# The first modulation in four parts instead of two, with c loaded and turned by itself

## The chip, the cores and the metric

One core of one Trainium2 chip runs the whole program in one launch. The metric is the device time in microseconds. Engines: PE multiplies, DVE, ACT and POOL work element by element, SP only issues transfers; transfers are also issued from ACT.

## What is computed

Two layers of a transformer on 512 latent and 256 context tokens of 1024 features. Only the first lines of layer 0 matter here:

```python
ml = (jax.nn.silu(c) @ w_mod[i] + b_mod[i])[:, None, :]
mc = jax.nn.silu(c_ctx) @ w_mod[i] + b_mod[i]
sh1, sc1, gt1, sh2, sc2, gt2 = jnp.split(ml, 6, axis=-1)
csh1, csc1, cgt1, csh2, csc2, cgt2 = jnp.split(mc, 6, axis=-1)
hl = rms_norm(xl, g_mix_pre[i]) * (1.0 + sc1) + sh1
hc = rms_norm(xc, g_mix_pre[i]) * (1.0 + csc1) + csh1
```

After them `hl` and `hc` are multiplied by the input projection `ab_w_in`, whose first part here are the values of the gated linear attention ("v0").

## The kernel before

**Precision and weights.** All products of the layers are float32 made of three products in fp32r: high part by high part, high by low, low by high. A unit of weights (0.5 MB) is loaded by SP into `w_raw` (3 places), rounded by ACT into `w_hi` (L855), and the rest is taken by POOL, or for some units by DVE, into `w_lo` (L537). The helper `feed(s)` of an engine does this for all units up to s. The unit of the stage v0 with number u serves the feature groups k = 2u and 2u + 1.

**Head.** Tokens lie in 6 tiles of 128 rows (4 latent, 2 context) in `x_res`, loaded by two transfers (L997, L998). For each tile ACT sums the squares (L844), POOL takes the root, DVE scales into `xs` (L1217), PE turns it in 8 transposes (L1863), and ACT (L1010) and DVE (L1451) copy the turned tile from PSUM to `x_t`, which holds features on partitions: 8 groups k of 128 features.

**First modulation.** Shift and scale of the mixer (the first 2048 columns of `w_mod[0]`) come as 16 tiles m of 0.5 MB in `mod_early` (8 places). They are split in two halves of 512 features for shift and scale each. Half 0 is m = 0 to 7, each one block of 128 input features. `modulation_rows` (L1824) multiplies a tile by the two columns silu(c), silu(c_ctx) in `c_pad`; four column groups of PE give four rows of results in one bank. When a half is complete, ACT copies it (L867), `modulation_columns` (L1851) turns it in two transposes, and `modulation_half` on DVE adds the bias (L1463) and forms `pre_a` = (1 + scale) * gain (L1469). Then ACT writes `h_hi` (L1032), DVE the same unrounded into `xs` (L1478, `modulate`) and the difference into `h_lo` (L1485, `modulated_low`), group after group.

The small parameters (bias rows, gains, c, c_ctx) come through one buffer, `par_rows`, with 9 transfers on one semaphore `par_in`; PE turns them at once (L2019, L2020), DVE copies them, and ACT makes `c_pad` (L1006) from them, all ahead of the first square. Products that only keep PE busy (`keep_busy`, L2025) stand before and after the first columns.

**v0.** PE runs `v0_part` for k = 0 to 7 (first pass, 18 products of 512 columns each: 6 token tiles by three products, L2044), then the same 8 groups by 160 further columns (second pass). Between them stand the tiles of half 1, four after k = 0 and four after k = 1, and its columns after k = 2:

```python
for k in range(KT):
    v0_part(k, sp("v0") + k // 2, BV * (k % 2), BV, True, k % 2 == 1, lambda t: ps(t, 0, BV))
    if k < 2:
        modulation_rows(range(KT + 4 * k, KT + 4 * k + 4))
    if k == 2:
        modulation_columns(1)
```

DVE then casts masks (L1506, L1507) and multiplies and adds the 8 tiles of the third modulation, m = 16 to 23, which is 16 operations into `la` (L1305, L1308, `add_rows("v0")`). PE sums them over partitions after v0, while DVE takes `r_tok` and `a_v` from PSUM (L1512, L1514); with these the next stage, "in0", begins. Each engine runs its own list in order; the order is the order of the code in its block.

## Time and profile before

| | |
|---|---|
| median of 3 runs | 1710.32 us (1709.58 to 1711.84) |
| the profiled execution | 1710.0 us |
| its span | 1708.2 us |
| PE busy | 1659.3 us (97%) |
| DVE, ACT, POOL busy | 744.8, 643.2, 684.6 us |
| granted clock of PE, mean | 0.996 |

The profile is of one execution. Times in its rows count from the span's start. A row gives the start, the duration, the engine, the line, the operation and out<-in; in brackets how long the engine sat idle before and what ended that. An fp32 product by 256 columns leaves two records.

### The profile page before, as it was taken

The page shows a single profiled execution, that of the slowest core. Times are in us where ns is not written, and L with a number is a line of the kernel's source. Part 1 is how long each engine was busy: PE and PEld are TensorE (multiplying, and loading weights), DVE is VectorE, ACT ScalarE, POOL GpSimd, SP SyncE. Part 2 cuts the span into 40 slices and gives each one's busy share as a digit, 9 for nine tenths or more (in the row PEclk, how much of TensorE's full clock was granted, in tenths as well). Part 3 has the DMA queues.
Part 4 walks back from the last instruction along what each step waited for, and adds up shares of the span by engine and source line. Part 5 has one row for each costly group of instructions (what it writes and reads, how often), then busy time and mean ns, then how long its engine had stood idle before and what let it go on. Part 6 is the DMA issues. An engine that isn't in the chain of part 4 may idle for free.

```text
span 1708.2 us, 25721 instructions
## 1 busy us (share of the span) xinstructions
PE 1659.3 (97%) x10146; PEld 1383.5 (81%) x10146; DVE 744.8 (44%) x1147; ACT 643.2 (38%) x1118; POOL 684.6 (40%) x453
## 2 busy tenths in 40 slices
PE   6999999998999999999999999999999999999997
PEld 4868886787887887879999878887888888888885
DVE  4836557717598644404655320016762441011103
ACT  4242126726422122223555442236763422222221
POOL 2311232048554545545641142325433544444443
PEclk9999999999999999999999999999999999999999
DMA  9742201034565655534666627342002442333331
GB/s 357 255 121 79 49 15 50 2 86 124 160 198 190 220 151 183 169 99 123 174 173 189 189 84 130 90 117 69 2 2 62 136 146 89 111 99 99 96 102 62
DMA packets 211987, 207.17 MB, mean 121 GB/s; under 512 B 16262, under 2 KB 180636, under 8 KB 211612
## 3 DMA queue, kind: packets, MB, share of 16 engines
q1 hardware_dynamic: 199208, 165.53, 32.3%
q10 hardware_dynamic: 12660, 39.99, 7.6%
q8 instruction: 82, 1.34, 0.3%
q14 instruction: 37, 0.30, 0.1%
HBM read 203.37 MB, written 2.13 MB: 120 GB/s over the span
## 4 chain that ended last, share of the span: by engine, by line
PE 89%; DVE 3%; issue 2%; POOL 2%; ACT 2%; DMA 1%; SPq 0%; DVEq 0%; POOLq 0%; ACTq 0%
PE ps L1746 45%; PE ps L1773 26%; PE ps L1929 3%; PE ps L1985 3%; PE ps L2044 3%; PE ps L1950 3%; POOL w_lo L537 2%; PE ps L1863 1%; PE ps L1824 1%; PE ps L1997 1%; ACT w_hi L855 1%; PE ps L2025 1%; DVE full L1257 1%; DMA mod_early<-in_w_mod 1%; ACT prob L957 1%
## 5 line engine op out<-in xcount | busy, mean ns | idle before, releaser
L537 POOL TENSOR_TENSOR w_lo<-w_raw,w_hi 128x1024 fp32r<-128x1024 f32 (+1 forms) x220 | 561.1, 2553 | 850.3 <-ACT w_hi L855 850.1
L1746 PE MATMUL ps<-h_hi,w_hi 128*128 128x512 f32 (+1 forms) x1488 | 496.0, 352 | 5.2 <-POOL w_lo L537 5.1
L1746 PE MATMUL ps<-h_hi,w_lo 128*128 128x512 f32 (+1 forms) x1488 | 491.6, 349 | 0.0
L1746 PE MATMUL ps<-h_lo,w_hi 128*128 128x512 f32 (+1 forms) x1488 | 490.6, 348 | 0.0
L855 ACT ACTIVATE w_hi<-w_raw 128x1024 fp32r<-128x1024 f32 (+1 forms) x273 | 286.6, 1051 | 329.4 <-PE ps L1773 282.4
L1746 PEld LDWEIGHTS ps<-h_hi,w_hi 128*128 128x128 f32 x1488 | 269.6, 189 | 49.0 <-issue 12.8
L1746 PEld LDWEIGHTS ps<-h_hi,w_lo 128*128 128x128 f32 x1488 | 269.3, 189 | 36.4
L1746 PEld LDWEIGHTS ps<-h_lo,w_hi 128*128 128x128 f32 x1488 | 269.3, 189 | 35.9
L537 DVE TENSOR_TENSOR w_lo<-w_raw,w_hi 128x1024 fp32r<-128x1024 f32 x53 | 69.7, 1316 | 195.4 <-ACT w_hi L855 195.4
L1327 DVE TENSOR_TENSOR hid_f<-silu_g,ps 128x512 f32<-128x512 f32 (+1 forms) x66 | 39.3, 595 | 253.4 <-PE ps L1746 252.9
L1773 PE MATMUL ps<-w_hi,hid_hi 128*128 128x512 f32 x440 | 136.1, 390 | 1.5 <-POOL w_lo L537 1.0
L1773 PE MATMUL ps<-w_hi,hid_lo 128*128 128x512 f32 x440 | 135.5, 389 | 0.0
L1773 PE MATMUL ps<-w_lo,hid_hi 128*128 128x512 f32 x440 | 135.5, 389 | 0.0
L928 ACT ACTIVATE hid_hi<-hid_f 128x512 fp32r<-128x512 f32 (+1 forms) x66 | 37.0, 560 | 240.9 <-DVE hid_f L1327 240.9
L1773 PEld LDWEIGHTS ps<-w_hi,hid_hi 128*128 128x128 f32 x440 | 82.2, 188 | 20.3 <-issue 2.2
L1773 PEld LDWEIGHTS ps<-w_lo,hid_hi 128*128 128x128 f32 x440 | 82.6, 188 | 17.2
L1773 PEld LDWEIGHTS ps<-w_hi,hid_lo 128*128 128x128 f32 x440 | 82.6, 188 | 17.1
L922 ACT ACTIVATE silu_g<-ps 128x512 f32<-128x512 f32 (+1 forms) x66 | 34.6, 524 | 145.0 <-PE ps L1746 144.7
L957 ACT ACTIVATE prob<-prob,negm 128x512 f32<-128x512 f32 (+2 forms) x112 | 78.2, 699 | 28.0 <-DVE negm L1367 19.1
L1773 PE MATMUL ps<-w_hi,h_hi 128*128 128x512 f32 x256 | 80.0, 394 | 3.3 <-POOL w_lo L537 3.3
L1773 PE MATMUL ps<-w_lo,h_hi 128*128 128x512 f32 x256 | 78.9, 390 | 0.0
L1773 PE MATMUL ps<-w_hi,h_lo 128*128 128x512 f32 x256 | 78.9, 389 | 0.0
(228 smaller groups left out, 1916.4 us busy)
## 6 DMA issues: line engine op xcount, KB each, us to landing
w_raw<-in_w_ffn_in SPq DMA_DIRECT2D x132, 512.0 KB, 3.9
w_raw<-in_w_ffn_out SPq DMA_DIRECT2D x66, 512.0 KB, 3.6
mod_raw<-in_w_mod ACTq DMA_DIRECT2D x42, 512.0 KB, 4.6
w_raw<-in_na_w_in SPq DMA_DIRECT2D x32, 512.0 KB, 3.8
mod_early<-in_w_mod SPq DMA_DIRECT2D x30, 512.0 KB, 10.5
full<-in_w_mod ACTq DMA_DIRECT2D x15, 512.0 KB, 5.3
w_raw<-in_ab_w_in SPq DMA_DIRECT2D x18, 256.0 KB, 7.5
w_raw<-in_ab_w_in SPq DMA_DIRECT2D x9, 512.0 KB, 4.3
```

Of the source, the lines that this page charges most:

```text
L537: eng.tensor_tensor(w_lo[:, u % RING, 0:width], w_raw[:, u % RAW, 0:width], w_hi[:, u % RING, 0:width].bitcast(F32), ALU.subtract).then_in ...
L855: act.activation(w_hi[:, u % RING, 0:width], w_raw[:, u % RAW, 0:width], ACT.Copy).then_inc(w_hi_done, 1)
L922: act.activation(silu_g[:, f % 2, 0:width], ps(2 * (f % 2), 0, width), ACT.Silu)\
L928: act.activation(hid_hi[:, j * width:(j + 1) * width], hid_f[:, f % 2, 0:width], ACT.Copy)\
L957: act.activation(prob[:, p % 2, x, 0:n], prob[:, p % 2, x, 0:n], ACT.Exp, bias=negm[:, c % 2, head:head + 1], scale=SCALE if layer == 0 el ...
L1327: dve.tensor_tensor(hid_f[:, f % 2, 0:width], silu_g[:, f % 2, 0:width], ps(2 * (f % 2) + 1, 0, width), ALU.mult).then_inc(ff_full, 1)
L1746: mm = pe.matmul(o[0], sta(x, o), mov(y, o), start=first and n == 0, stop=last and n == 2)
L1773: mm = pe.matmul(o, act(x, k, t), w[y][:, c:c + n], start=k == 0 and (x, y) == ("hi", "hi") and first_in_bank(name, i, c), stop=k == n_uni ...
L1929: mm = pe.matmul(ps(scores_bank(layer, p, x), at, at + width), q, kk[:, col:col + width], start=at % 512 == 0, stop=i == len(runs[x]) - 1, ...
L1950: mm = pe.transpose(ps(4 + x, j * P, (j + 1) * P), probs(p, x, j), ident[:])
L1985: mm = pe.matmul(ps(bank, at, at + P, 64 * x, 64 * x + 64), value_tile(p, x, j), turned_probs(layer, p)[:, x, j * P:(j + 1) * P], start=j ...
L2044: mm = pe.matmul(place(t), h_act(x, k, t), w[y][:, at:at + width], start=k == 0 and (x, y) == ("hi", "hi") and (first or t in (0, 3)), sto ...
```

## The change

`QT` = 4 quarters of 256 features for shift and scale each take the place of two halves. A tile m of a quarter holds two blocks of 128 input features (a "pair"), loaded by two transfers whose contiguous pieces are 1 KB instead of 2 KB. Quarter 0 (m = 0 to 3) is loaded first of all on SP's queue and used in the head, between the turned tiles; quarters 1 to 3 are loaded before units 1 to 3 and multiplied after k = 0, 2 and 4. Their columns stand inside k = 1, 3 and 5, before the third token tile. Each bank now holds two partial sums per result, so the turn is a product by a part of the identity that adds them: four products with 64 columns for two transposes. On ACT the copy of a quarter stands ahead of the rounding of the next unit. c and c_ctx get a buffer `c_rows`, their own transfers, issued first on ACT's queue, and their own turn; the other parameters are turned at the head's end. Tokens come in six transfers, one per tile, each with its own semaphore. The sink's copy and the w_lo of unit 0 move back on DVE. `nth(b)` only renumbers the waits of the later modulations. The core of the diff:

```diff
+QT = 4
...
             if m < 2 * KT:
-                both = a["w_mod"][0, k * P:(k + 1) * P, 0:2 * D].rearrange("p (i h n) -> p i h n", i=2, h=2)
-                eng.dma_start(mod_place(m).rearrange("p (i n) -> p i n", i=2), both[:, :, b])\
-                    .then_inc(mod_landing(m)[0], 16)
+                q, pair = divmod(m, QT)
+                rows = a["w_mod"][0, 2 * pair * P:2 * (pair + 1) * P, 0:2 * D].rearrange("(r p) (i q n) -> q p r i n", p=P, i=2, q=QT)
+                dst = mod_place(m).rearrange("p (r i n) -> p r i n", r=2, i=2)
+                for r in range(2):
...
             sync.dma_start(ident[:], a["k_ident"]).then_inc(ident_in, 16)
+            for m in range(QT):
+                mod_load(sync, m)
...
-            for src in (a["c"].rearrange("b (r n) -> (b r) n", n=P), a["c_ctx"].rearrange("(r n) -> r n", n=P)):
-                sync.dma_start(par_rows[at:at + KT, 1, :], src).then_inc(par_in, 16)
-                at += KT
-            sync.dma_start(sink[:], a["a_sink"].partition_broadcast(P)).then_inc(par_in, 16)
-            for m in range(KT):
-                mod_load(sync, m)
+            sync.dma_start(sink[:], a["a_sink"].partition_broadcast(P)).then_inc(sink_in, 16)
             for u, parts in enumerate(units):
-                if u in (sp("v0") + 1, sp("v0") + 2):
-                    first = KT + 4 * (u - sp("v0") - 1)
-                    for m in range(first, first + 4):
+                if sp("v0") < u < sp("v0") + QT:
+                    for m in range(QT * (u - sp("v0")), QT * (u - sp("v0") + 1)):
                         mod_load(sync, m)
-                if u == sp("v0") + RAW:
+                if u == sp("v0") + QT:
                     for dst, src in ((mask_in[:, 0:LT * 2 * P], a["k_near"]), (mask_in[:, LT * 2 * P:], a["k_window"]),
                                      (tri[:].rearrange("p a n -> p (a n)"), a["k_tri"])):
...
+            def quarter_copy(q):
+                act.wait_ge(mod_used, rows_done(QT * (q + 1) - 1))
+                if q >= 2:
+                    act.wait_ge(mod_turned, q - 1)
+                act.activation(gate_b[:, q % 2, 0:256], ps(6 + (q > 0), 0, 256), ACT.Copy).then_inc(mod_copied, 1)
...
-            act.dma_start(x_res[:, 0:LT, :], a["x"][0].rearrange("(t p) d -> p t d", p=P)).then_inc(x_in, 16)
-            act.dma_start(x_res[:, LT:NT, :], a["ctx"][0].rearrange("(t p) d -> p t d", p=P)).then_inc(ctx_in, 16)
+            act.dma_start(c_rows[0:KT], a["c"].rearrange("b (r n) -> (b r) n", n=P)).then_inc(c_in, 16)
+            act.dma_start(c_rows[KT:2 * KT], a["c_ctx"].rearrange("(r n) -> r n", n=P)).then_inc(c_in, 16)
+            for t in range(NT):
+                act.dma_start(x_res[:, t, :], a["x"][0, t * P:(t + 1) * P] if t < LT else a["ctx"][0, (t - LT) * P:(t - LT + 1) * P])\
+                    .then_inc(x_in[t], 16)
...
-            act.wait_ge(par_done, 1)
+            act.wait_ge(c_turned, 1)
             act.wait_ge(c_zero, 1)
-            act.activation(c_pad[:, :, 0:2], par_col[:, 68:84].rearrange("p (v k) -> p k v", v=2), ACT.Silu)\
+            act.activation(c_pad[:, :, 0:2], ps(5, 0, 2 * KT).rearrange("p (v k) -> p k v", v=2), ACT.Silu)\
                 .then_inc(c_done, 1)
...
-                pre_square("mix0", i, range(NT), (x_in, 16) if i < LT else (ctx_in, 16))
+                pre_square("mix0", i, range(NT), (x_in[i], 16))
                 if i >= 3:
                     take_turned(i - 3)
             take_turned(3)
             take_turned(4)
+            take_turned(5)
+            quarter_copy(0)
             feed(sp("v0"))
-            take_turned(5)
-            mod_copy(0)
             act.wait_ge(pre_half, NT)
             act.wait_ge(pre_full, NT)
             for k in range(KT):
-                if k == KT // 2:
-                    mod_copy(1)
-                if k in (0, KT // 2):
-                    act.wait_ge(mod_done, 1 if k == 0 else 2)
-                    act.wait_ge(*(mod_half, 1) if k == 0 else (mod_der, 1))
+                if k % 2 == 0:
+                    act.wait_ge(mod_done, k // 2 + 1)
+                    act.wait_ge(*(mod_half, k // 2 + 1) if k < KT - 2 else (mod_der, 1))
                 for lc, cols in enumerate((slice(0, SEQ), slice(SEQ, TOK))):
                     last = act.activation(h_hi[:, k, cols], x_t[:, k, cols], ACT.Identity,
                                           bias=mod_col[:, 0, lc, k:k + 1], scale=pre_a[:, 0, lc, k:k + 1])
                 last.then_inc(*(x_hi, 1) if k < KT - 1 else (pre_hi, NT))
-                if k in (1, 3):
+                if k % 2 == 1 and k < KT - 1:
+                    quarter_copy(k // 2 + 1)
                     feed(sp("v0") + 1 + k // 2)
 
             feed(sp("in0") + 1)
...
-            dve.wait_ge(par_in, 16 * 9)
-            dve.tensor_scalar(nsink[:], sink[:], -1.0, None, ALU.mult)
-            dve.wait_ge(par_turned, 2)
-            dve.tensor_copy(bias_col[:], ps(6, 0, 96))
-            dve.tensor_copy(par_col[:], ps(7, 0, 84)).then_inc(par_done, 1)
-            dve.wait_ge(par_done, 1)
...
-            feed(sp("v0"))
+            dve.wait_ge(par_turned, 2)
+            dve.tensor_copy(bias_col[:], ps(7, 0, 96))
+            dve.tensor_copy(par_col[:], ps(1, 0, 68)).then_inc(par_done, 1)
+            dve.wait_ge(par_done, 1)
+            def quarter(q):
+                dve.wait_ge(mod_turned, q + 1)
+                rows = ps(6 * (q > 0), 0, P).rearrange("p (j i v) -> p i v j", j=2, i=2)[:, :, 0:2]
+                cols = slice(2 * q, 2 * q + 2)
+                for i in range(2):
+                    bias = bias_col[:, i * KT + 2 * q:i * KT + 2 * q + 2]
+                    bias = bass.AP(bias.tensor, bias.offset, [list(bias.ap[0]), [0, 2], [1, 2]])
+                    last = dve.tensor_tensor(mod_col[:, i, :, cols], rows[:, i], bias, ALU.add)
                 last.then_inc(mod_done, 1)
...
+                dve.wait_ge(mod_done, q + 1)
+                gain = par_col[:, cols]
+                gain = bass.AP(gain.tensor, gain.offset, [list(gain.ap[0]), [0, 2], [1, 2]])
                 dve.scalar_tensor_tensor(pre_a[:, 0, :, cols], mod_col[:, 1, :, cols], 1.0, gain, ALU.add,
-                                         ALU.mult).then_inc((mod_half, mod_der)[h], 1)
-
-            modulation_half(0)
+                                         ALU.mult).then_inc(mod_half if q < QT - 1 else mod_der, 1)
+            quarter(0)
...
-            dve.wait_ge(mod_done, 1)
-            dve.wait_ge(mod_half, 1)
             for k in range(KT + 1):
-                if k == KT // 2:
+                if k == 1:
+                    feed(sp("v0"))
+                if k:
                     modulated_low(k - 1)
-                    modulation_half(1)
-                    dve.wait_ge(mod_done, 2)
-                    dve.wait_ge(mod_der, 1)
-                if k == 1:
-                    modulated_low(0)
+                if k and k < KT and k % 2 == 0:
+                    quarter(k // 2)
+                if k < KT and k % 2 == 0:
+                    dve.wait_ge(mod_done, k // 2 + 1)
+                    dve.wait_ge(*(mod_half, k // 2 + 1) if k < KT - 2 else (mod_der, 1))
                 if k < KT:
                     modulate(k)
-                if k > 1 and k != KT // 2:
-                    modulated_low(k - 1)
+            dve.wait_ge(sink_in, 16)
+            dve.tensor_scalar(nsink[:], sink[:], -1.0, None, ALU.mult)
             dve.wait_ge(consts_in, 16 * 3)
             dve.tensor_copy(window_b[:], mask_in[:, LT * 2 * P:])
             dve.tensor_copy(near_b[:].rearrange("p t n -> p (t n)"), mask_in[:, 0:LT * 2 * P]).then_inc(masks_done, 1)
...
+            def quarter_rows(q, pairs):
+                bank = 6 + (q > 0)
+                for pair in pairs:
+                    m = QT * q + pair
+                    if pair == 0:
+                        claim(bank)
+                    pe.wait_ge(*mod_landing(m))
+                    for g in range(4):
+                        mm = pe.matmul(ps(bank, 0, 256, 32 * g, 32 * g + 32), c_pad[:, 2 * pair + g // 2, :],
+                                       mod_place(m)[:, 256 * g:256 * g + 256], start=pair == 0, stop=pair == QT - 1,
+                                       skip_group_check=True)
+                    mm.then_inc(mod_used, 1)
+                if pairs[-1] == QT - 1:
+                    read_by((bank,), (mod_copied, q + 1))
+            def quarter_columns(q):
+                bank = 6 * (q > 0)
+                claim(bank)
+                pe.wait_ge(mod_copied, q + 1)
+                for j in range(2):
+                    for r in range(2):
+                        mm = pe.matmul(ps(bank, 64 * j, 64 * j + 64), gate_b[:, q % 2, j * P:(j + 1) * P],
+                                       ident[:, 64 * r:64 * r + 64], start=r == 0, stop=r == 1, skip_group_check=True)
+                mm.then_inc(mod_turned, 1)
+                read_by((bank,), (mod_done, q + 1))
 
             def modulation_sum(b):
...
-            pe.wait_ge(par_in, 16 * 9)
             pe.wait_ge(ident_in, 16)
-            pe.transpose(ps(6, 0, 96), par_rows[0:96, 0, :], ident[0:96, 0:96]).then_inc(par_turned, 1)
-            pe.transpose(ps(7, 0, 84), par_rows[0:84, 1, :], ident[0:84, 0:84]).then_inc(par_turned, 1)
-            read_by((6, 7), (par_done, 1))
+            pe.wait_ge(c_in, 32)
+            pe.transpose(ps(5, 0, 2 * KT), c_rows[0:2 * KT], ident[0:2 * KT, 0:2 * KT]).then_inc(c_turned, 1)
+            read_by((5,), (c_done, 1))
             pe.wait_ge(c_done, 1)
             def keep_busy(bank, n):
...
-            for m in range(KT):
-                modulation_rows([m])
-                if 1 <= m <= NT:
-                    pre_turn("mix0", [m - 1])
+            for pair, turned_tiles in enumerate(((0, 1, 2), (3,), (4,), (5,))):
+                pre_turn("mix0", turned_tiles)
+                quarter_rows(0, [pair])
+            pe.wait_ge(par_in, 16 * 6)
+            pe.transpose(ps(7, 0, 96), par_rows[0:96, 0, :], ident[0:96, 0:96]).then_inc(par_turned, 1)
+            pe.transpose(ps(1, 0, 68), par_rows[0:68, 1, :], ident[0:68, 0:68]).then_inc(par_turned, 1)
+            read_by((7, 1), (par_done, 1))
             claim(7)
             keep_busy(7, 3)
-            modulation_columns(0)
+            quarter_columns(0)
...
+                    if first and k % 2 == 1 and k < KT - 1 and t == 2:
+                        quarter_columns(k // 2 + 1)
...
                 v0_part(k, sp("v0") + k // 2, BV * (k % 2), BV, True, k % 2 == 1, lambda t: ps(t, 0, BV))
-                if k < 2:
-                    modulation_rows(range(KT + 4 * k, KT + 4 * k + 4))
-                if k == 2:
-                    modulation_columns(1)
+                if k % 2 == 0 and k < KT - 2:
+                    quarter_rows(k // 2 + 1, range(QT))
```

The places, as each engine's list has them. On PE, the columns of the second part of the modulation: `ps` is PSUM, `gate_b` the copied rows, `mod_early` the modulation tiles. Before, after k = 2:

```order
L2044 MATMUL ps<-w_hi,h_lo 128x512
L1851 MATMUL ps<-ident,gate_b 128x128 x2
L2044 MATMUL ps<-w_hi,h_hi 128x512
L2044 MATMUL ps<-w_lo,h_hi 128x512
L2044 MATMUL ps<-w_hi,h_lo 128x512
```

Now, from the end of k = 0 (the value product is L2085):

```order
L1849 MATMUL ps<-mod_early,c_pad 32x256 x16
L2085 MATMUL ps<-w_hi,h_hi 128x512
L2085 MATMUL ps<-w_lo,h_hi 128x512
L2085 MATMUL ps<-w_hi,h_lo 128x512
L2085 MATMUL ps<-w_hi,h_hi 128x512
L2085 MATMUL ps<-w_lo,h_hi 128x512
L2085 MATMUL ps<-w_hi,h_lo 128x512
L1863 MATMUL ps<-ident,gate_b 128x64 x4
```

The columns moved from between two steps into the step that follows their rows, behind two token tiles, and there are three such places.

On DVE, the end of the head and the first feature groups, before:

```order
L1451 COPY x_t<-ps 128x4x128 x2
L537 TENSOR_TENSOR w_lo<-w_raw,w_hi 128x1024
L1463 TENSOR_TENSOR mod_col<-ps,bias_col 128x2x4 x2
L1469 SCALAR_TENSOR_TENSOR pre_a<-mod_col,par_col 128x2x4
L1478 TENSOR_SCALAR xs<-x_t,pre_a,mod_col 128x512
L1478 TENSOR_SCALAR xs<-x_t,pre_a,mod_col 128x256
L1485 TENSOR_TENSOR h_lo<-xs,h_hi 128x768
```

and now, up to the second quarter:

```order
L1462 COPY bias_col<-ps 128x96
L1463 COPY par_col<-ps 128x68
L1473 TENSOR_TENSOR mod_col<-ps,bias_col 128x2x2 x2
L1478 SCALAR_TENSOR_TENSOR pre_a<-mod_col,par_col 128x2x2
L1487 TENSOR_SCALAR xs<-x_t,pre_a,mod_col 128x512
L1487 TENSOR_SCALAR xs<-x_t,pre_a,mod_col 128x256
L547 TENSOR_TENSOR w_lo<-w_raw,w_hi 128x1024
L1494 TENSOR_TENSOR h_lo<-xs,h_hi 128x768
```

The parameters' copies moved from the start of the list to behind the last turned tile, and w_lo from ahead of the modulation to between the first modulated group and its h_lo.

On ACT, the first feature groups, before and then now:

```order
L1032 ACTIVATE h_hi<-x_t,mod_col,pre_a 128x512
L1032 ACTIVATE h_hi<-x_t,mod_col,pre_a 128x256
L855 ACTIVATE w_hi<-w_raw 128x1024
L1032 ACTIVATE h_hi<-x_t,mod_col,pre_a 128x512
L1032 ACTIVATE h_hi<-x_t,mod_col,pre_a 128x256
```

```order
L1044 ACTIVATE h_hi<-x_t,mod_col,pre_a 128x512
L1044 ACTIVATE h_hi<-x_t,mod_col,pre_a 128x256
L878 ACTIVATE gate_b<-ps 128x256
L861 ACTIVATE w_hi<-w_raw 128x1024
L1044 ACTIVATE h_hi<-x_t,mod_col,pre_a 128x512
```

The rounding of the next unit now stands behind the copy of a quarter, so behind PE's tiles of it.

## Rows read from the trace of the kernel before

**Rows 1.** The page's first part: busy us and share of the span, by engine.

```profile
PE 1659.3 (97%) x10146; PEld 1383.5 (81%) x10146; DVE 744.8 (44%) x1147; ACT 643.2 (38%) x1118; POOL 684.6 (40%) x453
```

**Rows 2.** The chain that ended last, to 120 us: start, us, what.

```profile
27.51 1.49 PE ps L2025 x6
...
36.78 1.86 PE ps L1824 x32
...
38.64 4.30 PE ps L2044 x18
...
49.12 0.22 PE ps L1851 x2
...
49.34 36.49 PE ps L2044 x234
```

**Rows 3.** Timeline, PE: the first value product.

```profile
32.33 0.58 PE L2044 MATMUL ps<-w_hi,h_hi 128*128 128x512 f32 x1
```

**Rows 4.** Timeline, DVE: the sums of the third modulation and what follows.

```profile
57.90 4.85 DVE L1305 TENSOR_SCALAR la<-mod_early,c_pad 128x1024 f32<-128x1024 f32 x2
...
62.67 22.39 DVE L1308 SCALAR_TENSOR_TENSOR la<-mod_early,c_pad,la 128x1024 f32<-128x1024 f32 x14
...
85.85 0.42 DVE L1512 COPY r_tok<-ps 128x96 f32<-128x96 f32 x2 [0.78 <-PE ps L2044]
```

**Rows 5.** Timeline, ACT: table load, squares, copies, rounding, h_hi.

```profile
4.45 1.28 ACT L1006 ACT_TABLE_LOAD   x1 [4.45 <-issue]
...
13.00 1.04 ACT L844 ACTIVATE junk<-x_res 128x1024 bf16<-128x1024 f32 x1
...
15.46 1.06 ACT L844 ACTIVATE junk<-x_res 128x1024 bf16<-128x1024 f32 x1
...
20.60 0.60 ACT L1010 ACTIVATE x_t<-ps 128x512 f32<-128x512 f32 x1 [0.16 <-PE ps L1863]
...
27.57 0.39 ACT L867 ACTIVATE gate_b<-ps 128x256 f32<-128x256 f32 x1
...
29.81 2.50 ACT L1032 ACTIVATE h_hi<-x_t,mod_col,pre_a 128x512 fp32r<-128x512 f32 x4 [1.85 <-DVE pre_a L1469]
...
33.48 1.06 ACT L855 ACTIVATE w_hi<-w_raw 128x1024 fp32r<-128x1024 f32 x1 [1.16 <-DMA w_raw<-in_ab_w_in]
```

**Rows 6.** DMA queues from 6 to 8 us: packets, MB, share of 16 engines.

```profile
q10 hardware_dynamic: 187, 0.75, 92.2%
...
q1 hardware_dynamic: 173, 0.05, 10.4%
```

**Rows 7.** Timeline, PE transposes; then 14 to 19 us: busy by engine, PEclk, DMA share, GB/s.

```profile
16.80 1.97 PE L1863 MATMUL ps<-ident,xs 128*128 128x128 f32 x8
...
19.47 1.09 PE L1863 MATMUL ps<-ident,xs 128*128 128x128 f32 x8
...
14.00:19.00 5.00, 4.29 (x28) 2.20 (x32) 1.70 (x3) 3.77 (x9) 3.86 (x8) 1.00 1.05 387
```

**Rows 8.** Timeline, DVE: first unit's w_lo, and modulated groups.

```profile
27.59 1.22 DVE L537 TENSOR_TENSOR w_lo<-w_raw,w_hi 128x1024 fp32r<-128x1024 f32 x1
...
29.83 0.87 DVE L1478 TENSOR_SCALAR xs<-x_t,pre_a,mod_col 128x512 f32<-128x512 f32 x2
...
31.22 0.96 DVE L1485 TENSOR_TENSOR h_lo<-xs,h_hi 128x768 fp32r<-128x768 f32 x1 [0.52 <-ACT h_hi L1032]
...
34.64 2.98 DVE L1478 TENSOR_SCALAR xs<-x_t,pre_a,mod_col 128x512 f32<-128x512 f32 x2
```

**Rows 9.** Timeline, POOL: w_lo of weight units.

```profile
34.62 2.40 POOL L537 TENSOR_TENSOR w_lo<-w_raw,w_hi 128x1024 fp32r<-128x1024 f32 x1 [11.03 <-ACT w_hi L855]
...
55.85 6.36 POOL L537 TENSOR_TENSOR w_lo<-w_raw,w_hi 128x1024 fp32r<-128x1024 f32 x2 [12.08 <-ACT w_hi L855]
```

**Rows 10.** Lines L1364 and L1305 of DVE: duration ns min/median/max.

```profile
L1364 DVE SCALAR_TENSOR_TENSOR negm<-raw_max,nsink x24: 161/161/890, 260.1 to 337.0; 128x2 f32<-128x2 f32 x24
...
L1305 DVE TENSOR_SCALAR xs<-mod_raw,c_pad x6: 746/750/2900, 454.6 to 1360.0; 128x1024 f32<-128x1024 f32 x6
```

49 lines of the change are left out of this document (21 added, 28 removed).

## The prediction

> **What bounds the kernel now.** I read the page's engine line first: PE is busy for 97% of the span [rows 1], so only stretches where PE waits, or works on something other than the products, can give time back. The chain of waits then shows the place of the change [rows 2]. Behind the tokens' transposes and the first weight tiles it is PE itself: 1.49 us of keep-busy products that begin at 27.51, when the last weight tile of the first modulation half has been multiplied, and the first value product at 32.33 [rows 3]. From there PE never waits until 85.83: value steps of 4.30 us (18 products) alternate with groups of 1.86 us (four modulation tiles), and from 49.34 on 36.49 us follow without a gap: five more steps at 4.1, to 69.8, and the second pass over the narrow columns, 16.0. At 85.85 comes a short turn over DVE (r_tok), after which the stage "in0" starts. I call the time of the first value product T: 32.33 us before.
>
> What matters for the change is how near DVE is to being late. Its 16 sums for the third modulation (la<-mod_early) start at 57.90, as soon as the modulated tiles are done, and end at 62.67 + 22.39 = 85.06, only 0.8 us before PE wants DVE at 85.85 [rows 4]. So DVE has no slack at the end of this stage, though it is busy for only 44% of the span [rows 1].
>
> **The head, up to T.** c no longer waits for the small parameters: its two 4 KB transfers are issued first. ACT then issues 6 token transfers at 0.5 us and the four gw ones (all six of before were issued when the table load began at 4.45); so I put this load (1.28 us) at 6.0 and the first square near 7.5, against 13.00 [rows 5]. Tiles: while both queues had work (6 to 8 us) the token queue moved 0.75 MB in 187 packets and the other 0.05 MB in 173, about one packet each in turn [rows 6]. Token packets stay 4 KB; the modulation packets are now 1 KB. I estimate four fifths of 387 GB/s [rows 7] for tokens: 0.52 MB in 1.7 us, first tile at 6 us, sixth near 14.5, and the 2 MB of quarter 0 at about 18.
>
> ACT's floor is 6 squares at 1.23 us (13.00 to 15.46 for two) plus 6 copies of 0.60 = 11.0 us, so 18.5. The loop over DVE and PE took 1.6 us per tile before; here the first tile is scaled at about 9.7, the first transposes take 1.97 us instead of 1.09 [rows 5, 7], and DVE needs 1.5 us per tile. I get 21.9 for the end of the last quarter-0 tile, with 18.6 as floor and 24.3 if all transposes take the slow price. From there before needed 32.33 - 27.51 = 4.8 us. New on this path: the parameter transposes and their two copies, which now stand behind the sixth tile (0.4 + 0.5 us, and 0.1 of semaphores: 1.0); column products instead of two transposes (+0.7, below); and w_lo of the first weight unit, 1.22 us on DVE, now stands between the first modulation and h_lo, where DVE had idled 0.52 (+0.7) [rows 8]. T = 21.9 + 4.8 + 2.4 = **29.1, 3.2 us earlier** (25.5 to 31.5).
>
> **The columns.** Two transposes cost PE 0.22 us [rows 2]. They become four fp32 products with 64 moving columns, three times inside the value steps. Not shown anywhere: from below 4 x 0.11 = 0.44 us; from above 8 records at the 0.25 us of the keep-busy products (six records in 1.49, with 256 columns) = 2.0. With a quarter of those columns the lower end is the nearer row; I take 0.9.
>
> **The value steps.** Call r the time at which the four tiles of a quarter are multiplied. Before, k = 0 and its group ended at 36.78 + 1.86, so r1 = T + 6.3 [rows 2]. After r, PE does two tiles of the odd step (1.4), the columns (0.9 + 0.1), four tiles (2.7): it is at the next even step at r + 5.1. ACT: copy 0.39, then w_hi of the next unit 1.06, so POOL starts that unit's w_lo at r + 1.6 and ends it at r + 4.0 (2.40 us) [rows 5, 8, 9]. In this window the columns come out (r + 2.4) and DVE must add the bias, form pre_a, modulate and subtract. What POOL does to DVE then is in the trace: the modulation of one feature group takes 0.87 us alone and took 2.98 when it started at 34.64, 0.02 us behind a w_lo on POOL; it ended with it [rows 8, 9]. Small ones too: the fused operation on raw_max and nsink takes 161 ns and once 890 [rows 10]. So I let pre_a, which reads two SBUF tiles, wait until r + 4.0: pre_a at r + 4.15, h_hi on ACT 1.25 us (2.50 for two groups), h_lo 0.96 [rows 5, 8], with 0.3 of semaphores: PE can start the even step at r + 6.65 and has stood idle 1.55 us. The Trainium skill, SBUF - State Buffer, section Who interferes with whom, says the same of this case: a VectorE instruction with two SBUF inputs, or in a two-port mode, and GpSimd lock each other out for a whole instruction; one that reads PSUM and one SBUF tile doesn't, which would leave the bias sums free. By this rule the sum is as it stands; without it for the small operation, it is rival (a).
>
> An even step with its group takes 4.30 + 1.86 us [rows 2]. So r2 = T + 19.1, r3 = T + 32.0, the last even step starts at T + 38.7, and the first pass ends at T + 46.9. Before: 69.8 - 32.33 = 37.5. **+9.4 us**, of which 1.9 is the group that was in the head, 2.5 the columns (3 x 0.9 - 0.2), 4.65 the three idle stretches, 0.35 switches between shapes. The second pass (16.0 us) is unchanged and ends at T + 62.9.
>
> **DVE at the end.** The last modulated group is done at r3 + 8.35 = T + 40.4; before it was T + 24.4, 1.15 us ahead of the sums. Sink and mask casts: 1.15. The sums took 27.2 us, and the first two of them 4.85, where such a sum takes 0.75 alone [rows 4, 10]: 3.35 us were lost to the w_lo that start at 55.85 [rows 9]; those now lie mostly ahead of the sums, so 23.8. They end at T + 65.4, 2.5 behind PE's second pass. Counted from before (DVE's 85.85): T + 65.4 - 85.85 = T - 20.4, which with T = 29.1 is **+8.7**: -3.2 head, +9.4 first pass, +2.5 DVE late. Behind this point nothing changes: the queues of SP, ACT and POOL keep their order, w_raw of the next stage is free when PE's uses are, and all of it shifts along.
>
> **What costs nothing.** The loads of quarters 1 to 3: each is 2 MB and a weight unit of 0.5, 6.5 us at 387 GB/s [rows 7], and the steps between two quarters cover 12.9; uncovered, each would cost its lateness in full, since PE stands at the group. SP now holds the last tiles of the third modulation until quarter 3 is used; issued by T + 34 and landed by T + 41, they are summed after T + 50. The parameters' transfers stand behind quarter 0 on SP's queue; what they are late beyond 19 us would come on top of T.
>
> **Rivals.** (a) The small fused operation isn't held by POOL, only the modulation. Most of the fused ones on small tiles show 161 ns [rows 10]. Then ACT starts its h_hi at r + 2.95 and PE stands 0.25 us instead of 1.55; three of these are 3.9 us less: **+4.8**. (b) DVE's sums are not late, because POOL's w_lo fall elsewhere, on top of (a): 2.5 less, **+2.3**. (c) The head doesn't get shorter: tokens and weights share one bandwidth, and PE, waiting between tiles, works at the slow price until T: last tile at 24.3, keep-busy 1.3 us longer, T = 32.8: **+12.4**. For it: the first eight transposes took 1.97 us and later ones 1.09, although the granted clock is 1.00 (2.4 GHz) in that stretch [rows 7]. The Trainium skill, TensorE: Matmul & The Clock Gate, Part 1, has the array start at half clock and rise only once it is kept busy, which speaks against a head whose PE work is spread out. (d) The other side: the head ends at ACT's floor. Place: the squares and copies; price: last tile at 18.6, and parameters turned and first w_lo hidden in DVE's gaps, so T = 18.6 + 4.8 + 0.7 = 24.1, 8.2 us earlier. With the waits of my sum that is still +3.7. Without the three idle stretches and with DVE in time the steps add PE's bare work, 4.75 us, and the head decides: the point is T = 27.6, and T = 24.1 gives **-3.5**. Against it: DVE's own 1.5 us per tile, and w_lo's place in its queue.
>
> **Numbers.** The sums go against the profiled execution: 1710.0 us, 1.8 more than its span and 0.3 under the median of the three runs, 1710.32. Forecast 1710.0 + 8.7 = **1718.7**. Chances: main case 0.58, (a) 0.16, (b) 0.07, (c) 0.13, (d) 0.06. About 0.2%, 3.4 us, is what a measurement of this kernel can tell from no change. Main and (c) are slower nearly always, (a) mostly; (b), part of (a) and half of (d) fall within. Faster 0.06, same 0.14, slower 0.80. Range: from (a) and (b) with an early T to (c): 1711.8 to 1723.5.
>
> **What would show it.** First value product near 29 us; three idle stretches of PE of 1.5 us ahead of k = 2, 4, 6, ended by h_lo; pre_a starting with POOL's w_lo running and lasting over 1 us; the DVE sums ending near T + 65 and PE waiting about 2.5 us for them. T below 25, no wait ahead of the even steps, or sums that end before PE's second pass would each make it wrong.

## The result and the profile after

| | before | after |
|---|---|---|
| median | 1711.08 us (1709.58 to 1713.67, 4 runs) | 1723.89 us (1722.4 to 1723.94, 4 runs) |
| ratio | | 1.0073 [1.0061, 1.0085] |
| profiled execution | 1710.0 us, span 1708.2 | 1723.94 us, span 1722.1 |
| granted clock, mean | 0.996 | 0.994 |

The change made the kernel 12.8 us slower. The forecast was +8.7; the measured 1723.89 lies 0.4 us above the upper end of its range, 1723.5. In later comparisons the kernel before had medians of 1711.33, 1710.37, 1711.71 and 1710.91 us. The profiled execution of a variant (b_hid) ran at a granted clock of 0.85 nearly throughout; it is left out of that variant's time, and another profiled execution of the same kernel (b_hid_again) is read in its place.

PE's line of the page, after, against [rows 1]:

```profile
PE 1669.2 (97%) x10175; PEld 1389.9 (81%) x10175; DVE 746.6 (43%) x1153; ACT 643.9 (37%) x1120; POOL 683.6 (40%) x453
```

PE worked 9.9 us more. Products at half clock count as busy, so this is not 9.9 us of new work.

The head and the first even step, timeline of PE, after (against [rows 2, 3]):

```profile
21.02 0.64 PE L1849 MATMUL ps<-mod_early,c_pad 128*32 128x256 f32 x8
...
22.44 1.56 PE L2061 MATMUL ps<-x_res,ident 128*128 128x256 f32 x6 [0.48 <-DVE par_col L1463]
23.84 1.00 PE L1863 MATMUL ps<-ident,gate_b 128*128 128x64 f32 x8
...
28.44 0.50 PE L2085 MATMUL ps<-w_hi,h_hi 128*128 128x512 f32 x1
...
41.08 0.50 PE L2085 MATMUL ps<-w_hi,h_hi 128*128 128x512 f32 x1 [1.16 <-DVE h_lo L1494]
```

T, the start of the first value product, is 28.44; the wait ahead of k = 2 is the 1.16 us in brackets of the last line. Behind it stands what DVE and POOL did (timelines of DVE and of POOL, after, against [rows 8, 9]):

```profile
37.14 0.23 DVE L1473 TENSOR_TENSOR mod_col<-ps,bias_col 128x4 f32<-128x4 f32 x2 [6.98 <-PE ps L1863]
37.41 1.16 DVE L1478 SCALAR_TENSOR_TENSOR pre_a<-mod_col,par_col 128x4 f32<-128x4 f32 x1
38.66 0.87 DVE L1487 TENSOR_SCALAR xs<-x_t,pre_a,mod_col 128x512 f32<-128x512 f32 x2
40.07 0.96 DVE L1494 TENSOR_TENSOR h_lo<-xs,h_hi 128x768 fp32r<-128x768 f32 x1 [0.54 <-ACT h_hi L1044]
```

```profile
36.16 2.38 POOL L547 TENSOR_TENSOR w_lo<-w_raw,w_hi 128x1024 fp32r<-128x1024 f32 x1 [18.42 <-ACT w_hi L861]
```

The bias sums, which read PSUM, take their usual time while POOL works. `pre_a`, over 4 elements per partition, lasts until POOL is done at 38.54. In the head it took 0.16 us.

The end of the stage, timeline of DVE, after (against [rows 4]):

```profile
67.22 2.35 DVE L1494 TENSOR_TENSOR h_lo<-xs,h_hi 128x768 fp32r<-128x768 f32 x1
69.49 0.16 DVE L1513 TENSOR_SCALAR nsink<-sink 128x8 f32<-128x8 f32 x1
69.56 0.61 DVE L1515 CAST window_b<-mask_in 128x896 bf16<-128x896 f32 x1
70.10 2.05 DVE L1516 CAST near_b<-mask_in 128x1024 bf16<-128x1024 f32 x1
72.07 1.41 DVE L1318 TENSOR_SCALAR la<-mod_early,c_pad 128x1024 f32<-128x1024 f32 x2
73.40 21.06 DVE L1321 SCALAR_TENSOR_TENSOR la<-mod_early,c_pad,la 128x1024 f32<-128x1024 f32 x14
94.39 0.41 DVE L1521 COPY r_tok<-ps 128x96 f32<-128x96 f32 x2
```

And what PE does then, in the chain of waits, after:

```profile
92.00 2.48 DVE la L1321 x2
94.47 0.14 issue
94.61 1.94 PE ps L1876 x16
96.55 2.05 PE ps L2108 x12
...
99.78 2.18 PE ps L2119 x4
101.96 5.72 PE ps L1755 x24
```

PE ended its second pass at 90.9 and stood 3.7 us. Up to here the shift is +8.5 us (r_tok at 94.39 for 85.85), close to the +8.7 of the prediction. But the pieces behind it are longer than in the kernel before. Its chain has for the last three:

```profile
87.34 1.48 PE ps L2069 x12
90.01 1.95 PE ps L2080 x4
91.96 4.44 PE ps L1746 x24
```

The stretches by window tell why; the columns are us, then busy time with its instructions for PE, PEld, DVE, ACT and POOL, then the granted clock, the DMA share and GB/s. After:

```profile
95.00:97.00 2.00, 2.00 (x20) 1.24 (x13) 0.72 (x2) 0.40 (x2) 0.00 (x0) 0.50 0.74 172
97.00:100.00 3.00, 1.80 (x11) 1.40 (x10) 1.01 (x2) 0.93 (x1) 1.99 (x1) 0.84 1.04 310
100.00:103.00 3.00, 3.00 (x7) 1.43 (x7) 2.03 (x4) 0.00 (x0) 0.35 (x1) 0.73 0.90 225
```

Before:

```profile
85.00:95.00 10.00, 8.27 (x57) 5.71 (x56) 5.09 (x11) 1.33 (x2) 2.34 (x1) 1.00 0.84 231
95.00:97.00 2.00, 2.00 (x21) 1.35 (x24) 0.00 (x0) 0.00 (x0) 0.00 (x0) 1.00 0.00 0
```

Behind the wait PE was granted half its clock (1.2 of 2.4 GHz) for two spells of 3.4 us; the clock's records in this trace have them from 94.5 and from 101.4 on.

To see where the rest came from, I took each product of PE and compared its start with that of the product that stands as many places from the end of PE's list in the kernel before. The table gives how much later it starts, in us, at five times of the kernel before (near 100, 540, 1090, 1455 and 1690 us), for all kernels that are read. T itself differs between executions of one program's head (31.6 to 33.0 us in those with the head of before, 27.7 to 28.5 in the changed one and those made from it), and that is part of each row:

| kernel | 100 | 540 | 1090 | 1455 | 1690 |
|---|---|---|---|---|---|
| after | 11.3 | 10.7 | 12.4 | 12.8 | 13.9 |
| a_busy | 8.6 | 7.9 | 9.5 | 9.9 | 10.9 |
| a_round | 9.4 | 9.0 | 10.7 | 10.4 | 11.5 |
| a_casts | 9.4 | 8.8 | 10.6 | 9.4 | 10.4 |
| a_all | 4.5 | 5.0 | 6.7 | 4.2 | 5.3 |
| after_w | 11.8 | 11.7 | 11.7 | 9.1 | 9.1 |
| a_sums_w | 3.6 | 4.0 | 4.0 | 4.0 | 4.0 |
| b_same | 0.1 | 0.1 | 0.1 | 0.1 | 0.1 |
| b_head | -2.2 | -1.7 | 0.0 | -2.5 | -1.5 |
| b_head_w | -2.1 | -2.1 | -2.2 | -2.2 | -2.2 |
| b_late | 8.0 | 7.8 | 8.8 | 9.7 | 9.7 |
| b_late_busy | 5.1 | 5.0 | 6.1 | 7.2 | 7.2 |
| b_late2 | -0.4 | 0.0 | -0.1 | 0.8 | 0.8 |
| b_pad | 3.6 | 3.2 | 8.2 | 8.1 | 11.3 |
| b_pad32 | 3.5 | 3.4 | 8.3 | 7.9 | 11.1 |
| b_hid_again | 3.4 | 3.4 | 9.3 | 8.1 | 11.2 |

For the changed kernel: +8.5 at r_tok, +2.8 by the clock, and then more that grows inside the feed-forward output stages ("fo", from 540 us on), where nothing waits and nothing was changed. Steps of about 0.9 or 1.7 us, as between 1090 and 1455 in several rows, are dips of the granted clock that one profiled execution has and another hasn't (before has one of 3.4 us at 1169 and one at 1330, after none at 1169 and 6.8 us at 1340).

### The profile page after: what moved, and what is told of

Read it like the earlier page. It is cut to its first block, busy times and chain, and to the rows that moved or that the text cites. A ratio compares the mean times of both kernels' runs of the same rounds, so it can differ in the third digit from the quotient of the medians.

```text
span 1722.1 us, 25818 instructions
## 1 busy us (share of the span) xinstructions
PE 1669.2 (97%) x10175; PEld 1389.9 (81%) x10175; DVE 746.6 (43%) x1153; ACT 643.9 (37%) x1120; POOL 683.6 (40%) x453
## 4 chain that ended last, share of the span: by engine, by line
PE 85%; DVE 4%; issue 3%; POOL 2%; ACT 2%; DVEq 0%; POOLq 0%; ACTq 0%
PE ps L1755 45%; PE ps L1782 26%; PE ps L1966 3%; PE ps L2022 3%; PE ps L1987 2%; POOL w_lo L547 2%; DVE la L1321 1%; PE ps L1900 1%; PE ps L2034 1%; ACT w_hi L861 1%; ACT prob L968 1%; DVE full L1270 1%; DVE prob L1372 0%; PE ps L1833 0%; ACT junk L850 0%
## 5 line engine op out<-in xcount | busy, mean ns | idle before, releaser
L968 ACT ACTIVATE prob<-prob,negm 128x512 f32<-128x512 f32 (+2 forms) x112 | 78.1, 699 | 28.5 <-DVE negm L1380 19.6
```

Source lines behind the costliest of these rows:

```text
L968: act.activation(prob[:, p % 2, x, 0:n], prob[:, p % 2, x, 0:n], ACT.Exp, bias=negm[:, c % 2, head:head + 1], scale=SCALE if layer == 0 el ...
```

## The experiments

Names that begin with a are made from the changed kernel, those with b from the kernel before.

### The wait for DVE and the clock behind it

**a_busy**: 8 products that only keep PE busy ahead of the sum of the third modulation.

```diff
             read_by((6, 7), (v_dve, 2))
+            claim(0)
+            keep_busy(0, 8)
             modulation_sum(2)
```

> The changed kernel with eight keep-busy products (256 columns, 3.5 us by the row 3.67 us for sixteen records) in PE's list ahead of the sum of the third modulation, that is, in the 3.7 us in which PE waits for DVE's sums. Theory: the wait itself costs about 3.7 us and, because PE stood still, its clock is granted at half for 3.4 us at 94.5 and again at 101.4; that second part is worth 2.7 us (sum 1.94 instead of 1.07, turn of r_tok 2.05 instead of 1.48, first unit of in0 5.72 instead of 4.44). With the products the clock stays at full: 1721.2 us, DVE's sums ending where they did (94.5). Rival: the clock falls for another reason or the slower pieces are not its doing: 1723.9, unchanged; if the products run into the sums' end, up to 1724.5.

Measured: 1722.76 us, ratio 1.0055 [1.0042, 1.0067]. Timeline of PE, a_busy:

```profile
90.80 3.65 PE L2061 MATMUL ps<-x_res,ident 128*128 128x256 f32 x16
94.69 1.07 PE L1876 MATMUL ps<-la,one_hot 128*32 128x256 f32 x16 [0.24 <-DVE la L1321]
95.95 1.47 PE L2110 MATMUL ps<-ident,r_tok 128*32 128x128 f32 x12 [0.19 <-DVE a_v L1523]
98.61 1.95 PE L2121 MATMUL ps<-gw,r_t 33*128 33x512 f32 x4 [1.19 <-DVE r_t L1526]
```

DVE is as late as in the changed kernel, but the wait is filled, every piece behind it has its length of before, and the shift at 100 us is 2.7 us smaller. The median fell by only 1.1, and the intervals of the two ratios (this one and 1.0061 to 1.0085) overlap: the profile shows the 2.7 us, the timed runs alone don't.

**b_late** and **b_late_busy**: the kernel before with a late DVE, without and with the filling.

```diff
             dve.wait_ge(consts_in, 16 * 3)
+            for i in range(6):
+                dve.tensor_copy(window_b[:], mask_in[:, LT * 2 * P:]).then_inc(again, 1)
+                dve.wait_ge(again, i + 1)
             dve.tensor_copy(window_b[:], mask_in[:, LT * 2 * P:])
```

> The kernel before with six more copies of window_b on DVE ahead of the sums (same results). DVE's sums should end near 88.8 us instead of 85.06, so PE stands about 3 us ahead of the sum of the third modulation. Theory A (a wait of PE of this length makes the granted clock fall, wherever it comes from): the clock is at 0.50 for about 3.4 us once or twice within 15 us behind the wait, PE's pieces between 89 and 110 us take 2.7 us more than in before, and the shift at 110 us is +5.7. Theory B (the clock fell in the changed kernel because of its three idle stretches and its spread work in the first pass, not because of the wait): clock 1.00 there, shift at 110 us +3.0. Time: by A 1711.3 + 5.7 = 1717.0, by B 1714.3; 2.2 more in both if the 229 ns pitch of the later stages comes with every edit.

> The same with eight products that only keep PE busy (2 us) ahead of the sum of the third modulation, so that DVE is as late but PE stands about 1 us instead of 3. Theory A: no fall of the granted clock between 89 and 110 us, shift at 110 us +3.0, 2.7 less than without the eight products. Theory B: no difference from the kernel without them, both at +3.0. Time by A 1714.3, or 1716.5 with the pitch of 229 ns.

Measured: b_late 1718.49 us, ratio 1.0042 [1.0027, 1.0058]; b_late_busy 1714.12 us, 1.0025 [1.0015, 1.0035]. r_tok of b_late is at 88.83, +3.0 as expected. The chain of waits, b_late:

```profile
89.06 1.94 PE ps L1843 x16
91.00 2.53 PE ps L2073 x12
94.70 3.75 PE ps L2084 x4
98.45 5.90 PE ps L1750 x24
```

Its stretch by window:

```profile
90.00:95.00 5.00, 3.81 (x25) 2.58 (x18) 1.19 (x3) 1.33 (x2) 2.34 (x1) 0.50 1.01 283
```

The clock fell although the first pass is that of before, so the three idle stretches aren't needed for it (theory B falls). It stayed at 0.50 for 13.7 us from 88.1 on and took 5.0 us, not 2.7. With the filling PE no longer stood ahead of the sum, and the shift at 100 us is 5.1 instead of 8.0: 2.9 us less, or 3.5 when T, which was 0.6 later in this execution, is taken off. But against the expectation b_late_busy too had one spell of 3.4 us at half clock, at 95.9.

**b_late2**: two copies instead of six.

> The kernel before with two more copies of window_b on DVE ahead of the sums. The sums should end near 86.4 us and PE wait about 0.5 us for them, r_tok +0.5. If every lateness of DVE makes the clock fall: 0.50 for 3.4 us or more between 86 and 100 us, shift at 110 us +2.2 or more. If only a wait of microseconds does: clock 1.00, shift +0.5, total 1711.8 beside a before of 1711.2.

Measured: 1711.22 us, ratio 1.0002 [0.9993, 1.0011]. PE stood 0.6 us ahead of the sum, no fall of the clock behind it. T was 31.6 in this execution for 32.3, so the shift is -0.4. A short lateness costs itself and no more.

Does the wait make the clock fall, always and alone? The mean granted clock of every timed run says more than one profile; (1 - clock) times the span is the time for which the half was missing. The clock of a run is recorded to 0.001, which is 1.7 us here, so only means say something. As means over the runs of each kernel:

| PE's wait ahead of the sum | missing, us |
|---|---|
| 2.5 us or more: after, after_w, a_round, a_casts, b_late | 11.6, 12.0, 12.0, 11.0, 15.0 |
| 0.6 us or less: a_busy, a_all, a_sums_w, b_head, b_head_w, b_late_busy, b_late2, b_pad, b_pad32, b_hid | 9.3, 7.2, 9.8, 6.4, 9.0, 9.2, 8.0, 8.1, 9.0, 7.9 |
| the kernel before (four comparisons) | 8.9, 7.8, 9.0, 8.4 |

Five of five with the wait lie above all the others; single runs of the two groups overlap (8.6 to 15.5 us against 5.1 to 12.0). It is not the only cause of a fall: b_pad, b_pad32, b_hid_again and a_sums_w had one between 91 and 98 us in their profiled execution with no longer wait than before. What decides there I can't tell. Over all timed runs b_pad, b_pad32 and b_hid miss no more clock than the kernel before does, so nothing shows that this fall belongs to these kernels.

### The three idle stretches

**a_round**: on ACT the rounding of the next unit ahead of the quarter's copy, so that POOL's w_lo comes earlier.

```diff
                 if k % 2 == 1 and k < KT - 1:
-                    quarter_copy(k // 2 + 1)
                     feed(sp("v0") + 1 + k // 2)
+                    quarter_copy(k // 2 + 1)
```

> The changed kernel with one thing moved: ACT rounds the weight unit ahead of the copy of the quarter instead of behind it, so POOL takes w_lo while DVE has nothing to do, and not over pre_a. Theory (POOL's w_lo holds pre_a, 1.16 us instead of 0.16, and so ACT and h_lo): pre_a back to 0.16 us in all quarters, PE's three idle stretches of 1.15 us ahead of k = 2, 4, 6 shrink to 0.1 to 0.3, DVE's sums end 3.0 to 3.3 us earlier, the wait for them stays at 3.7 us: about 1720.7 us. Rival: the stretches come from the chain columns, bias, h_hi, h_lo itself and stay near 1.1: 1723.5 to 1724.

Measured: 1719.6 us, ratio 1.0044 [1.0031, 1.0056], r_tok at 91.32. Timelines of POOL and of DVE, a_round:

```profile
29.66 2.74 POOL L547 TENSOR_TENSOR w_lo<-w_raw,w_hi 128x1024 fp32r<-128x1024 f32 x1 [11.56 <-ACT w_hi L861]
```

```profile
37.39 0.16 DVE L1478 SCALAR_TENSOR_TENSOR pre_a<-mod_col,par_col 128x4 f32<-128x4 f32 x1
```

With POOL done at 32.4, `pre_a` is back at 0.16 us in all quarters, and r_tok comes 3.1 us earlier, 1.0 per quarter. This shows the hold, and its price.

### DVE's lateness

**a_casts**: the mask casts behind the copies of r_t.

```diff
-            dve.wait_ge(consts_in, 16 * 3)
-            dve.tensor_copy(window_b[:], mask_in[:, LT * 2 * P:])
-            dve.tensor_copy(near_b[:].rearrange("p t n -> p (t n)"), mask_in[:, 0:LT * 2 * P]).then_inc(masks_done, 1)
             add_rows("v0")
...
             dve.tensor_copy(r_t[0:32, SEQ:], ps(2, 0, CTX, 0, 32)).then_inc(r_in, 1)
+            dve.wait_ge(consts_in, 16 * 3)
+            dve.tensor_copy(window_b[:], mask_in[:, LT * 2 * P:])
+            dve.tensor_copy(near_b[:].rearrange("p t n -> p (t n)"), mask_in[:, 0:LT * 2 * P]).then_inc(masks_done, 1)
```

> The changed kernel with DVE's two mask casts (2.6 us with their waits for POOL, 69.56 to 72.15) moved from ahead of the sixteen sums to behind the copies of r_t. Theory: the sums end 2.6 us earlier, PE's wait goes from 3.7 to about 1.1 us, the clock does not fall, so 2.6 + 2.7 = 5.3 less: 1718.6 us. Rival (clock not tied to the wait): only 2.6 less, 1721.3. Rival (the wait is not DVE's list but the landing of the tiles): no change, 1723.9.

Measured: 1722.4 us, ratio 1.0055 [1.0042, 1.0067]: a miss. r_tok is at 92.49, but T was 0.8 earlier in this execution, so the casts gave only 1.1 us. The small operation on `sink` that stands ahead of the sums was held by POOL's w_lo in place of the cast. Timelines of DVE and of POOL, a_casts:

```profile
68.72 1.53 DVE L1513 TENSOR_SCALAR nsink<-sink 128x8 f32<-128x8 f32 x1
```

```profile
68.25 1.97 POOL L547 TENSOR_TENSOR w_lo<-w_raw,w_hi 128x640 fp32r<-128x640 f32 x1 [0.26 <-ACT w_hi L861]
```

It had taken 0.16 us in the changed kernel. The sums themselves took 22.4 us in both. PE still stood 2.5 us, and the clock fell.

**a_all**: both moves, and 6 keep-busy products.

> The changed kernel with all three repairs: on ACT the rounding of the next unit ahead of the copy of a quarter, the mask casts behind r_t's copies, and six keep-busy products ahead of the sum of the third modulation. If the parts add as single runs gave them (rounding -3.1 us, casts -1.2 to -1.9, clock -2.8): 1723.9 - 7.1 = 1716.8, range 1715.5 to 1718, so still 5.5 us above before; r_tok at about 90 us instead of 94.4; no idle stretch of PE ahead of k = 2, 4, 6. The rival: the repairs overlap, since less waiting in the first pass brings PE to the sums earlier and DVE is then later for them by as much; then 1719 to 1720.

Measured: 1716.8 us, ratio 1.0031 [1.0019, 1.0044], r_tok at 90.40. The parts add up as expected.

**a_sums_w**: both moves, no keep-busy products; two of the eight tiles of sums go into DVE's idle time ahead of quarter 3, and 64 bytes of padding (see below).

```diff
                     modulated_low(k - 1)
+                if k == KT - 2:
+                    add_rows("v0", range(2 * KT, 2 * KT + 2))
                 if k and k < KT and k % 2 == 0:
                     quarter(k // 2)
...
-            add_rows("v0")
+            add_rows("v0", range(2 * KT + 2, 3 * KT))
```

> The changed kernel with the rounding ahead of a quarter's copy, the mask casts behind r_t's copies, the padding, and the first two of the eight tiles of sums moved into DVE's 7 us of idle time ahead of the last quarter (4.4 us of work); no keep-busy products. If DVE is late for no other reason, PE's wait ahead of the sum of the third modulation goes: r_tok at 90.4 - 3.1 = 87.3 us, no fall of the clock between 85 and 110 us, and the total is that of the version with all repairs, 1716.8, less 3.1 for the wait and 2.2 for the padding: 1711.5, range 1710.5 to 1713, level with before. Rival: the sums in the first pass share SBUF with POOL's w_lo and delay the next modulated group; then PE stands ahead of k = 6 and r_tok is at 88 to 89.

Measured: 1713.45 us, ratio 1.0008 [1.0, 1.0017], above the expected range (1710.5 to 1713); and the clock did fall, for 3.4 us at 94.7, without a wait ahead of the sum. Timeline of DVE, a_sums_w:

```profile
53.44 3.55 DVE L1319 TENSOR_SCALAR la<-mod_early,c_pad 128x1024 f32<-128x1024 f32 x2
56.92 2.47 DVE L1322 SCALAR_TENSOR_TENSOR la<-mod_early,c_pad,la 128x1024 f32<-128x1024 f32 x2
60.50 0.23 DVE L1474 TENSOR_TENSOR mod_col<-ps,bias_col 128x4 f32<-128x4 f32 x2 [1.12 <-PE ps L1866]
...
87.98 0.42 DVE L1521 COPY r_tok<-ps 128x96 f32<-128x96 f32 x2 [1.37 <-PE ps L2088]
```

The two tiles fit with 1.1 us to spare, and at the end DVE waits for PE again, as before. r_tok is at 87.98 and T at 28.46. From T to r_tok are 59.5 us, against 53.5 before: with nearly every wait repaired (0.2 us is left ahead of each even step), four parts cost PE 6.0 us more than two; 1.9 of them are the group of tiles that stood in the head before. That is the price of the idea itself. It buys 1.7 us in the head, as the next run shows.

### The head alone

**b_head**: the kernel before with the new head (c first, six token transfers, parameters turned at the end), but two halves. The edit is the part of the diff on these, with par_col at 68 columns and `c_rows`.

> The kernel before with the new head alone: c with its own transfers and turn, token tiles one by one, modulation tiles first on SP's queue, other parameters turned at the end of the head; halves, columns and the order of the value steps as before. Theory: first value product at 29.5 to 30.5 instead of 32.3 (bound by the 4 MB of half 0 beside 3 MB of tokens), everything behind it shifts along: 1708.5 us against 1711.1. Rival: the eighth modulation tile lands no earlier than before because the tokens take the bandwidth first, T at 32 or later: 1711 or more.

Measured: 1708.83 us, ratio 0.9988 [0.9979, 0.9998]. Timeline of PE, b_head:

```profile
30.13 0.58 PE L2051 MATMUL ps<-w_hi,h_hi 128*128 128x512 f32 x1
```

T is 30.13 for 32.33. So about 2.2 us of the gain in the head need no quarters.

### The slower products at 550 us

Every one of the first five kernels with the new head (after, a_busy, a_round, a_casts, b_head) spent about 0.55 us more in each of the five blocks of 264 fo products, with a pitch (median time from the start of one product to that of the next) of 229 ns instead of 227.

**b_same**: the kernel before once more, unchanged.

> The kernel before, unchanged, in one more profiled execution. It answers whether the pitch of the value and output products of the later stages (227 ns in the profile of before, 229 ns in the profiles of the changed kernel and of the four variants so far) belongs to the program or to the execution. Theory 1: any edit of the program brings 229 ns, so here it is 227 ns again, and the blocks of 264 products near 550 and 1460 us take 60.28 and 59.84 us within 0.1. Theory 2: it differs from execution to execution; then it can be 229 ns here too, and the blocks take 60.8 and 60.4. The time is that of the other runs of before, 1709 to 1714 us.

Measured: 1710.11 us. The chain of waits, b_same:

```profile
543.01 60.27 PE ps L1773 x264
```

The profiled execution of before had 60.28 here, and b_late, b_late_busy and b_late2, all edited, had 60.28 as well. So it is neither the execution nor just any edit. b_head has it, in its chain:

```profile
541.25 60.82 PE ps L1776 x264
```

What b_head shares with the changed kernel and not with b_late is the width of `par_col`, 68 columns for 84: all that is allocated behind it stands 64 bytes lower in each partition (`mask_in` apart, which shares its scope with the new `c_rows`).

**b_head_w** and **after_w**: b_head and the changed kernel with these 64 bytes given back. **b_pad**: the kernel before with the same edit, so 64 bytes higher. **b_pad32**: with 8 columns, 32 bytes.

```diff
         par_col = sb("par_col", [P, 68])
+        sb("pad", [P, 16])
```

> The kernel before with the new head alone (as in the variant with that head), and 64 bytes per partition of unused SBUF behind par_col, so that every tile allocated behind it (hid_hi, hid_lo, c_pad, the attention's tiles) has the address that it has in the kernel before. Theory C: the longer pitch of the products in the fo stages (229 ns for 227) comes from these addresses, which the change moved by 64 bytes when it cut par_col from 84 to 68 columns. Then the pitch is 227 again, the blocks of 264 products take 60.28 and 59.84 us, the total is 2.2 us below the variant without the pad, 1708.8 - 2.2 = 1706.6 beside a before of 1711.0, and the dips of the granted clock that go with the stage's timing may move too. Theory D: it comes from anything else in the new head (more semaphores, another program length): 229 ns stays, 1708.8.

> The changed kernel with the same 64 bytes of padding behind par_col. Theory C: fo blocks back at 60.28 and 59.84 us, total 1723.9 - 2.2 = 1721.7, all steps up to 110 us unchanged (T 28.4, three idle stretches of 1.15 us, wait of 3.7 us, clock at 0.50 behind it, shift +11.3). Theory D: 1723.9.

> The kernel before with 64 bytes per partition of unused SBUF behind par_col and nothing else: the tiles behind it stand 64 bytes higher. Theory C with an address rule of 128 bytes: the same pitch of 229 ns as 64 bytes lower, the blocks of 264 products take 60.8 and 60.4 us, total +2.2: 1713.2 beside a before of 1711.0. Theory C with another period, or theory D: 227 ns and 1711.0.

> The kernel before with 32 bytes per partition of unused SBUF behind par_col. If any displacement slows the products, the blocks of 264 take 60.8 to 62 us and the total is +2 to +8; if only an odd multiple of 64 bytes does, 60.28 us and 1711.

Measured: b_head_w 1709.02 us beside a before of 1711.71, ratio 0.9985 [0.9976, 0.9993], where 1706.6 was expected; after_w 1721.37, 1.0053 [1.004, 1.0066]; b_pad 1718.77, 1.0039 [1.0026, 1.0052], and b_pad32 1720.58, 1.0054 [1.0041, 1.0067], both above what was expected. With the addresses of before the blocks are back at 60.27 and 60.24 us, and the table's rows of b_head_w and a_sums_w are flat from 300 us on. Moved up, they get worse: b_pad, chain of waits:

```profile
546.10 61.97 PE ps L1774 x264
```

There is a block to compare with: 264 products of the same shape at 1096 us read `h_hi` and `h_lo`, which are allocated ahead of `par_col` and haven't moved. The chains of waits, before and then b_pad:

```profile
1096.44 59.85 PE ps L1773 x264
```

```profile
1104.65 59.85 PE ps L1774 x264
```

The changed kernel has 59.85 there too.

b_head_w's ratio is only 0.0003 under b_head's. In the trace b_head lost 2.8 us in its five blocks and gained 0.4 elsewhere (its shift goes from -2.2 to -2.6 between 100 and 200 us); but its timed runs missed 6.4 us of clock against 9.0. So the total of this pair doesn't show what the addresses cost; the blocks do.

**b_hid**: 64 bytes ahead of `hid_hi` alone, in the scope of the feed-forward. **b_hid_again**: the same kernel, profiled once more.

```diff
+            sb("pad", [P, 16], scope=s1)
             hid_hi = sb("hid_hi", [P, FH * SEQ], F32R, scope=s1)
```

> The kernel before with 64 bytes per partition of unused SBUF ahead of hid_hi, in the feed-forward scope alone: only hid_hi, hid_lo and the tiles allocated behind them there stand 64 bytes higher. Theory E (the address of the moving operand hid_hi, hid_lo against that of the weights decides the pitch): the pitch in the fo stages is 231 ns as with everything moved, the blocks of 264 products take 61.97 and 61.60 us, and nothing changes ahead of 500 us: clock 1.00 between 85 and 110 us. Total +7: 1718. Theory F (another tile, or the operands of DVE, ACT and POOL that work beside PE): blocks at 60.28 and 59.84 us, total as before.

> The same kernel as before with hid_hi and hid_lo 64 bytes higher, one more profiled execution at full clock. Theory E: pitch 231 to 235 ns in the fo stages, blocks of 264 products at 61.9 and 61.6 us, the product-by-product shift grows by about 1.7 us in each and stands at about +8 behind the last, with nothing ahead of 540 us. Theory F: 60.28 and 59.84 us.

Measured: b_hid 1719.2 us, ratio 1.0049 [1.0036, 1.0063]; b_hid_again 1721.47. The chain of waits, b_hid_again:

```profile
546.30 61.95 PE ps L1774 x264
```

Its windows:

```profile
90.00:95.00 5.00, 4.62 (x11) 2.56 (x12) 3.00 (x5) 0.00 (x0) 0.99 (x1) 0.66 0.87 231
```

The same lengths as with everything moved: what counts is where `hid_hi` and `hid_lo`, which these products read as moving operand, begin, or a tile that begins behind them in the same scope. No run separates the two; that it is the operand is argued from its being the only moved tile that PE reads there. A clock fall at 91.6 us came as well, against the expectation, though nothing that is used there has moved.

## Why the prediction was wrong

The forecast of the stage up to r_tok came out; what failed is the step behind it, "Behind this point nothing changes ... and all of it shifts along", and this in two ways: 2.8 us by a fall of the clock, and about 2.8 in the five fo blocks by moved addresses. Point by point:

- **The head.** T 28.44 for 29.1. Last tile of quarter 0 at 21.02 + 0.64 = 21.7 for 21.9. Table load at 6.66 for 6.0, first square at 8.04 for 7.5. Right. Rival (c), a slow head, did not happen. It was priced with the transposes of 1.97 us "although the granted clock is 1.00", which the row can't carry: the first record of the clock in the trace of before begins at 19.2 us, and a stretch without a record prints as 1.00. Eight transposes took 1.97 us ahead of 19.2 and 1.09 behind it; after has 5.28 us for three times eight from 11.03 on, its first record at 16.0, and 1.09 for eight from then on. Which level PE had earlier no record says. Of the 3.9 us gained, about 2.2 belong to the new order of loads and 1.7 to the smaller first part (b_head).
- **The columns.** 1.00 us busy, 0.8 until the next product, for 0.9. Right.
- **The hold by POOL.** `pre_a` lasted until the end of w_lo in all three quarters, and a_round took the hold away and with it 3.1 us. Right in mechanism, so rival (a) is out; the even step started at r + 6.4 (41.08, with r = 34.68) instead of r + 6.65, and the idle stretches are 1.15 us instead of 1.55. The Trainium skill, SBUF - State Buffer, section Who interferes with whom, had it so: the operation with two SBUF inputs was held, the bias sum with one in PSUM took 0.23 us for two as ever. In a_round, without the hold, PE still stands 0.16 us ahead of the even step; rival (a) had 0.25.
- **DVE late.** 3.7 us of PE idle for 2.5. The sums end at T + 66.0 for T + 65.4: the last h_lo (2.35 us) and the near_b cast (2.05) were held by POOL's w_lo, while the sums themselves took 22.4 us for 23.8. PE was done at T + 62.5 for T + 62.9.
- **The sum at r_tok: +8.5 for +8.7.** That it is so close is partly luck. Head, PE's two passes and the wait for DVE were -3.9, +9.0 and +3.5 for -3.2, +9.4 and +2.5, and the errors cancel. Within the passes the idle stretches were 1.2 us shorter than summed, and PE's own work 0.8 longer.
- **Behind r_tok, the clock.** Not in the sum at all. The wait, 2.5 us in the sum, was counted at its own length; it was 3.7 us and cost 2.8 more, because the granted clock fell to 0.50 behind it. The prediction used a slow PE only for the head, in rival (c).
- **Behind r_tok, the addresses.** Also not in the sum. The diff cuts `par_col` from 84 to 68 columns, which was read as bookkeeping. Between 540 and 1690 us the shift grows by 3.2, of which 2.8 in the five blocks of 264 fo products; with the 64 bytes given back they have their length of before. The median fell by 2.5 us (1721.37 for 1723.89), though the intervals of the two ratios overlap a little.

8.5 + 2.8 = 11.3 at 100 us, less 0.6 of quicker products up to 540 us (0.1 in after_w, so most of it goes with the addresses too), plus 3.2 up to 1690, is the 13.9 us between the two profiles. The medians differ by 12.8; the dips of the clock elsewhere vary between runs by more than that difference.

A version that beats both is b_head_w: the new head with two halves and the old addresses, 2.7 us under the kernel before (b_head, 2.5 us under, can't be told from it).

## What to carry to other kernels

A wait of PE can cost more than its length (2.5 to 3.7 us here, in five kernels of five, while 0.6 us cost nothing more): add what is lost at half clock behind it, or fill it with products that only keep PE busy, which gave 2.7 to 2.9 us back in the profile. Splitting a step to start earlier pays once, at the start, and costs PE at every piece: here 1.7 us gained, 6.0 paid (1.9 of them work that only changed its place). A tile whose width changes moves all tiles behind it; compare the pitch of the products in stages that the change doesn't touch, and put the old addresses back before judging the change.

## What the hardware showed that was not expected

- **The address of a moving operand changes the pitch of products.** With hid_hi and hid_lo at the addresses of before, the block of 264 products by 512 columns near 545 us takes 60.27 us; 64 bytes lower 60.8; 32 or 64 bytes higher 61.94 and 61.97 (61.95 with only these two and the tiles behind them in their scope moved). Over the five blocks this is 2.8 us in the first case by the traces (by the medians 2.5 between after and after_w, and nothing between b_head and b_head_w); in the others it is 7 to 10 us of the kernel by the medians. That the operand does it, and not a tile behind it in the scope, is argued, not shown. All of these are multiples of the element size, which is all that the Trainium skill, SBUF - State Buffer, section Operand start alignment, asks for; it says there that this is about legality, not speed. No rule for the good addresses came out of these four placements.
- **The granted clock falls after a wait in the middle of the program**, to 0.50 for 6.8 to 13.7 us in all (after, a_casts; a_round, after_w; b_late), and sometimes without one: for 3.4 us in a_sums_w and b_late_busy, and for 6.8 us with hid_hi moved, at 91.6 us, 450 us ahead of its first use. This second kind stays unexplained.
- **A DVE operation on 4 elements per partition lasted 1.16 us** while POOL's w_lo ran, and 0.16 without it; starting POOL's work 6.5 us earlier (29.66 for 36.16), without making any less of it, gave 3.1 us over three such places. `nsink`, over 8 elements, lasted 1.53 us in a_casts for 0.16.
